# Keys and values of the recurrence turned by VectorE and device memory instead of TensorE

## What is computed

```python
def wkv_scan(r, w, k, v, kk, a, s0, reverse):       # 16 heads of 64
    def step(S, inp):
        r_t, w_t, k_t, v_t, kk_t, a_t = inp
        sa = jnp.einsum("bhvk,bhk->bhv", S, kk_t)
        S = (S * w_t[:, :, None, :]
             - sa[..., None] * (kk_t * a_t)[:, :, None, :]
             + v_t[..., None] * k_t[:, :, None, :])
        return S, jnp.einsum("bhvk,bhk->bhv", S, r_t)
oc_f, sc_f = scan_direction(con, 0, s0, False)      # context, forwards
oc_b, sc_b = scan_direction(con, 1, s0, True)       # context, backwards
ol_f, _ = scan_direction(lat, 0, sc_f, False)       # latents go on from there
ol_b, _ = scan_direction(lat, 1, sc_b, True)
```

## Time and profile before

| | us |
|---|---|
| median of three executions | 2393.3 (2391.81 to 2393.4) |
| the profiled execution | 2391.25 |
| its span, first to last instruction | 2389.2 |
| TensorE busy in the span | 2357.6 (99%) |
| VectorE / ScalarE / GpSimd busy | 1526.6 (64%) / 558.5 (23%) / 419.0 (18%) |
| from the first transpose of turn 0 to that of turn 31 | 481.56 |

### The profile page before, as it was taken

The page is one execution under the profiler, slowest core; times in us unless marked ns, Lnnn a source line. Parts: engine busy times, 40 slices in busy tenths (PEclk is TensorE's granted clock), DMA queues, the critical chain, the costliest instruction groups (busy, mean ns, idle before and its releaser), DMA issues.

```text
span 2389.2 us, 54476 instructions
## 1 busy us (share of the span) xinstructions
PE 2357.6 (99%) x24052; PEld 2057.5 (86%) x24052; DVE 1526.6 (64%) x2964; ACT 558.5 (23%) x1289; POOL 419.0 (18%) x483
## 2 busy tenths in 40 slices
PE   8999999999999999999999999999999999999999
PEld 8999888899999998889999888488888888556558
DVE  7886674488778766744987887255555554147652
ACT  2101030111011010301111111245555554132341
POOL 1111000112011100001223320234444440100000
PEclk9999999999999999999999999999999999999999
DMA  7555544445545554545454322000000001212111
GB/s 282 185 180 193 190 178 153 165 161 205 197 162 193 178 194 176 184 151 179 176 193 162 112 80 71 1 3 3 3 3 3 3 3 38 89 53 88 53 53 71
DMA packets 40427, 285.03 MB, mean 119 GB/s; under 512 B 4544, under 2 KB 5744, under 8 KB 6272
## 3 DMA queue, kind: packets, MB, share of 16 engines
q1 hardware_dynamic: 36000, 252.83, 29.6%
q0 software_dynamic: 4192, 28.72, 3.3%
HBM read 280.48 MB, written 1.05 MB: 118 GB/s over the span
## 4 chain that ended last, share of the span: by engine, by line
PE 96%; DVE 2%; ACT 2%; issue 0%; DMA 0%; POOL 0%; SPq 0%; DVEq 0%; ACTq 0%; POOLq 0%
PE psum L696 27%; PE psum L1039 21%; PE psum L1100 12%; PE psum L1208 6%; PE psum L714 5%; PE psum L1338 4%; PE psum L1327 3%; PE psum L1340 2%; PE psum L1287 1%; PE psum L1427 1%; ACT arena L1957 1%; PE psum L1010 1%; PE psum L1274 1%; PE psum L1297 1%; PE psum L1411 1%; PE psum L1355 1%
## 5 line engine op out<-in xcount | busy, mean ns | idle before, releaser
L696 PE MATMUL psum<-arena,ring 128*128 128x256 f32 (+1 forms) x2864 | 675.2, 395 | 8.3 <-ACT arena L1735 8.0
L696 PEld LDWEIGHTS psum<-arena,ring 128*128 128x128 f32 x2864 | 541.8, 190 | 129.7 <-issue 56.5
L1039 PE MATMUL psum<-arena 128*128 128x128 f32 x2560 | 325.0, 275 | 0.0
L1039 PEld LDWEIGHTS psum<-arena 128*128 128x128 f32 x2560 | 305.1, 192 | 0.0
L1039 PE MATMUL psum<-arena,ring 128*128 128x128 f32 x1920 | 253.6, 275 | 0.0
L1039 PEld LDWEIGHTS psum<-arena,ring 128*128 128x128 f32 x1920 | 233.9, 192 | 0.2
L2348 DVE TENSOR_TENSOR arena<-ring 128x1024 f32<-128x1024 f32 x136 | 171.1, 1258 | 38.6 <-PE psum L1100 34.7
L1100 PE MATMUL psum<-arena 128*128 128x128 f32 x1408 | 184.6, 275 | 0.0
L1100 PEld LDWEIGHTS psum<-arena 128*128 128x128 f32 x1408 | 170.7, 192 | 0.0
L2370 DVE SCALAR_TENSOR_TENSOR arena<-arena 128x256 f32<-128x256 f32 x336 | 164.1, 530 | 5.2
L1338 PE MATMUL psum<-arena 64*64 64x64 f32 x2560 | 158.5, 223 | 0.9 <-DVE arena L2763 0.7
(11 more groups left out here) (343 smaller groups left out, 3373.1 us busy)
## 6 DMA issues: line engine op xcount, KB each, us to landing
ring<-in_weights SPq DMA_DIRECT2D x238, 1024.0 KB, 4.8
arena<-in_ada POOLq DMA_DIRECT2D x24, 1024.0 KB, 5.4
arena<-in_const POOLq DMA_DIRECT2D x1, 1312.0 KB, 6.4
arena<-in_x SPq DMA_DIRECT2D x1, 1024.0 KB, 4.8
ring<-in_weights SPq DMA_DIRECT2D x2, 512.0 KB, 6.7
arena<-in_ctx POOLq DMA_DIRECT2D x1, 1024.0 KB, 7.5
arena<-in_lora POOLq DMA_DIRECT2D x1, 1024.0 KB, 5.2
out<-arena SPq DMA_DIRECT2D x8, 128.0 KB, 1.9
```

Source lines behind the costliest of these rows:

```text
L696: mm = self.nc.tensor.matmul(out, self.ring[:, slot % RING, i * P:(i + 1) * P], rhs, start=(kc == 0), stop=(kc == len(moving) - 1))
L1039: mm = nc.tensor.matmul(bank[:, n * P:(n + 1) * P], left[:, kind, pair, :], right[:, pair, :], start=(n == 0 and pair == 0), stop=(n == la ...
```

## The change

VectorE turns the operands in squares of 32x32, and transfers through device memory bring the squares to their partitions.

- `turn_squares(q)` on VectorE: two directions, each one transpose of the keys (128x256) and one of the values (128x128), written to `squares_turned` with a step of four elements. The backward values are read backwards from `rkv`, so `v_rev`, `reverse_values` and the memset of its head are gone.
- Where: `turn_squares(0)` stands ahead of the loop. In turns with g other than 0, `turn_squares(q+1)` stands between `take_z` and `mask_lower(q+1, 2)`; with g = 0, after `sum_decays`, `mask_lower` and `update_state`, at the end of the turn. It waits until the squares of the turn before have been spilled.
- On SP, for each turn: four transfers of 32 partitions x 6 x 128 elements (98 KB each) to `squares_0` or `squares_1` in device memory, a wait for all four, then one of 128x512 elements (262 KB) to `bk_t` and one of 64x512 (131 KB) to `uv`. From turn 2 on the latter two wait for `os_full` of the turn two before.
- TensorE loses `turned_bk` and `turned_v`; `kv` waits for the values' transfer in place of ScalarE, and the first `out_and_state` of a turn has a wait for the keys' transfer added. ScalarE loses `take_turned_bk`, `take_turned_v` and `reverse_values`.
- `bk_t` and `uv` are now `[buffer, feature, unit]`: a matrix operand reads 64 columns with a step of four elements (16 bytes), and `take_u` writes so.
- The first weight loads over `bk` are issued from between the turns' transfers and wait for `squares_turned` and `stack_full`.

```diff
-    bk_t = second.take(2, 4, P)
-    uv = second.take(2, 4, P)
+    bk_t = second.take(2, P, 4)
+    uv = second.take(2, P, 4)
     kv_buf = (second.take(4 * HEAD), second.take(4 * HEAD))
+    squares_turned = Arena(arena, second.at).take(6, SQUARE, 4)
...
+            for q in range(TURNS):
+                b, n = q % 2, q // 2 + 1
+                if q >= 2:
+                    sp.wait_ge(s.bk_landed[b], 16 * (n - 1))
+                    sp.wait_ge(s.v_landed[b], 16 * (n - 1))
+                sp.wait_ge(s.squares_turned, q + 1)
+                for f in range(P // SQUARE):
+                    rows = slice(f * SQUARE, (f + 1) * SQUARE)
+                    sp.dma_start(spilled[b][:, :, f, :].rearrange("c i t -> i c t"),
+                                 squares_turned[rows, :, :, :].rearrange("p c j u -> p c (j u)"))\
+                        .then_inc(s.squares_spilled[b], 16)
+                sp.wait_ge(s.squares_spilled[b], 4 * 16 * n)
+                if q >= 2:
+                    sp.wait_ge(s.os_full, 2 * q - 2)
+                sp.dma_start(bk_t[:, b, :, :].rearrange("p f u -> p (f u)"),
+                             spilled[b][0:4].rearrange("c i f t -> (c i) (f t)")).then_inc(s.bk_landed[b], 16)
+                sp.dma_start(uv[CHUNK:P, b, :, :].rearrange("p f u -> p (f u)"),
+                             spilled[b][4:6].rearrange("c i f t -> (c i) (f t)")).then_inc(s.v_landed[b], 16)
+                for i in range(2):
+                    if q == TURNS - GROUPS + 1 + i:
+                        load_b(i)
+            for i in range(2, SECOND_B_SLOTS):
+                load_b(i)
...
-            def turned_bk(q):
-
-                pair, g = divmod(q, GROUPS)
-                out_ = st.bank(("bk_turned", q), 512)
-                for u in range(4):
-                    jj, d = divmod(u, 2)
-                    mm = nc.tensor.transpose(out_[:, u * P:(u + 1) * P], bk[:, pair % 2, d, 2 * g + jj, :], identity)
...
-                        pe.wait_ge(s.act_taken, SCAN.taken(("v_turned", q)))
+                        pe.wait_ge(s.v_landed[q % 2], 16 * (q // 2 + 1))
                         for u in range(4):
                             jj, d = divmod(u, 2)
                             for h in range(2):
                                 mm = mm_(out_[halves[h], u * HEAD:(u + 1) * HEAD], gram_at(q % 2, jj, d, h)[HEAD:P, 0:CHUNK],
-                                         uv[HEAD:P, q % 2, u, h * HEAD:(h + 1) * HEAD], start=True, stop=True)
+                                         uv[HEAD:P, q % 2, h * HEAD:(h + 1) * HEAD, u], start=True, stop=True)
...
+                if jj == 0:
+                    pe.wait_ge(s.bk_landed[par], 16 * (q // 2 + 1))
...
-                        mm_(ps_o[halves[h], d, :], uv[:, par, 2 * jj + d, h * HEAD:(h + 1) * HEAD],
+                        mm_(ps_o[halves[h], d, :], uv[:, par, h * HEAD:(h + 1) * HEAD, 2 * jj + d],
                             gram_at(par, jj, d, h)[:, CHUNK:], start=False, stop=True)
                 for d in range(2):
                     for h in range(2):
                         cols = slice(h * HEAD, (h + 1) * HEAD)
-                        mm = mm_(ps_s[halves[h], d, :], bk_t[:, par, 2 * jj + d, cols], uv[:, par, 2 * jj + d, cols],
+                        mm = mm_(ps_s[halves[h], d, :], bk_t[:, par, cols, 2 * jj + d], uv[:, par, cols, 2 * jj + d],
...
-                turned_bk(q)
-                turned_v(q)
...
-            def reverse_values(n):
-                nc.scalar.activation(v_rev[:, n % 2, CHUNK:].rearrange("p (s t) -> p s t", s=2),
-                                     rkv[:, 2 * DC + n, :].rearrange("p (s t) -> p s t", s=2)[:, :, ::-1],
-                                     ACT.Copy).then_inc(s.reversed_ready, 1)
...
-                        uv[0:CHUNK, q % 2, 2 * jj:2 * jj + 2, h * HEAD:(h + 1) * HEAD],
+                        uv[0:CHUNK, q % 2, h * HEAD:(h + 1) * HEAD, 2 * jj:2 * jj + 2].rearrange("p f u -> p u f"),
...
-                take_turned_bk(q)
-                take_turned_v(q)
...
+            def turn_squares(q):
+                pair, g = divmod(q, GROUPS)
+                if g == 0:
+                    dve.wait_ge(s.pair_ready, pairs_ready(pair, 1))
+                if q >= 1:
+                    dve.wait_ge(s.squares_spilled[(q - 1) % 2], 4 * 16 * ((q - 1) // 2 + 1))
+                stream, at = g // 2, g % 2 * 2 * CHUNK
+                for d in range(2):
+                    nc.vector.transpose(
+                        squares_turned[:, 0:4, :, d::2].rearrange("p c j u -> p u c j"),
+                        bk[:, pair % 2, d, 2 * g:2 * g + 2, :].rearrange("p u (c j) -> p u c j", j=SQUARE))
+                    values = rkv[:, 2 * DC + pair, stream * T:(stream + 1) * T]
+                    values = (values if d == 0 else values[:, ::-1])[:, at:at + 2 * CHUNK]
+                    ins = nc.vector.transpose(
+                        squares_turned[:, 4:6, :, d::2].rearrange("p c j u -> p u c j"),
+                        values.rearrange("p (u c j) -> p u c j", u=2, c=2))
+                ins.then_inc(s.squares_turned, 1)
...
+            dve.wait_ge(s.lora_in, 4)
+            turn_squares(0)
...
+                elif ahead:
+                    turn_squares(q + 1)
                if ahead:
                    mask_lower(q + 1, 2)
                 if k >= 0:
                     update_state(k + 1)
+                if q % GROUPS == 0 and q // GROUPS + 1 < PAIRS:
+                    turn_squares(q + 1)
```

54 lines of the change are left out of this document (15 added, 39 removed).

## The result

The changed kernel takes 2435.05 us (median of four executions, 2434.45 to 2435.51) and the kernel before 2393.35 beside it. The ratio is 1.0179, with a 95% interval from 1.0167 to 1.0191. The forecast was 2388.5 in a range from 2383 to 2420; the time lies 15 us above the range. It lies nearest to rival B's figure for the case that the stationary operands are held up too, 2432. Two executions far outside all others (3432.5 us of the version with six returns, 6007.1 us of the kernel before) count in no ratio of this document.

What follows compares the result with a forecast made beforehand. TensorE's queue plus its waits for short round trips through ScalarE or VectorE bound the recurrence; -4.4 + 0.6 = -3.8 us gives 2387.4 from 2391.25 and 2389.5 from the median, middle 2388.5, range 2383 to 2420.

Steps and rivals of the forecast that it cites:

- rival B: TensorE's stepped operand reads take twice as long: 2418 us for moving operands, 2432 with stationary ones too; chance 0.26.
- the stride: TensorE operands read a float32 every 16 bytes, 48 passes a turn; ends zero and 44 us, taken as zero.
- GpSimd sets the pace: In 12 turns with g = 1 and 2, GpSimd's preparation of the next pair holds up the mask; no gain counted.
- The cover: Before lower_product(q, 4), removed transposes mostly covered ScalarE's copy; 0.23 of 1.03 us gained in 19 turns, 4.4 us.
- Turn 1: ScalarE comes late from a table load and exponentials, and lower_product follows it with or without transposes; nothing gained.
- The first turn: turn_squares(0) stands ahead of the mask, so TensorE goes on at 1556.12; 0.6 us lost, once.
- VectorE's transposes: Four a turn ahead of mask_lower(q+1, 2) take 1.4 us, ends 0.9 and 2.2, hidden in 2.3 us of room.
- rival C: VectorE's transposes don't fit and wait for GpSimd, losing 1.3 us in 14 turns: 18 us, 2407; chance 0.11.
- The transfers: Spill and return take 6.7 us, at worst 9.6, against 12.0 us from squares to kv at g = 1; zero cost.
- Rival D: Transfers land late for kv, over 12 us after turning; at 14 us seven g = 1 turns lose 2 each: 2402; chance 0.05.

Runs made afterwards that it cites:

- version with six returns: Layout by unit with each turn's two returns from device memory issued as six, one per square of tokens; 2390.4 us, ratio 0.9991 to the kernel before.
- all accesses in a row: Changed kernel with TensorE's reads of bk_t and uv and ScalarE's writes of u on neighbouring elements, values wrong; 2389.7 us, ratio 0.999 to the kernel before.
- without squares and transfers: Changed kernel with all accesses in a row, VectorE's squares and the transfers left out, values wrong; 2389.7 us, ratio 0.9989 to the kernel before.
- squares made twice: Version with six returns, with VectorE's four transposes a turn made a second time into unread memory; 2389.5 us, ratio 0.999 to the kernel before.
- layout by unit: Changed kernel with bk_t and uv kept as [buffer, unit, feature], the spill scattering 128-byte pieces; 2407.5 us, ratio 1.0064 to the kernel before.

## Why the prediction was wrong

One term of the sum was wrong, and it was as large as the whole result.

**The step that failed** is the stride: ends of zero and 44 us, zero taken. It measured 45.5 us (2435.1 against 2389.6). The reason given for zero was two rows of eight elements, a memset on VectorE, which only writes, and a small ScalarE instruction, on other engines, with a step of 256 bytes, and so short that a start-up cost of 59 or some 200 ns hides a few ns. They could not bear the choice, and the text said as much; the honest use of rows that don't reach the question is to leave both ends standing. The range did not: it cut half of rival B away to 2420, below its own figure of 2432 for the case that came. With 26% on B and a bound of 44 us, the range should have ended beyond 2432.

Rival B's price was nearly right. It took twice the time for each of 48 passes a turn, 29 ns a pass; 26 were measured for kv and for L1437. Measured from the first start of a group to whatever TensorE starts next, which takes in its last pass, kv holds the queue for 1.08 us instead of 0.59, and the two groups of `out_and_state` for 1.14 instead of 0.62 (medians): 32 x 0.49 + 64 x 0.52 = 49 us. The six turns with g = 2 in which GpSimd sets the pace gave back 0.6 us each, 3.6 in all, since TensorE's wait behind it (0.53 us in turn 14 with all accesses in a row) is gone from them in the changed kernel. That leaves 45.5 us (by unrounded medians), as much as was measured. Smaller differences (turn 2, and a stretch at half clock that the changed kernel's profile has more, told below) were not followed one by one.

**The cover** was right. TensorE waits for ScalarE's copy in place of the transposes, 0.69 us in a turn. A stretch from one `lower_product(q, 5)` to the next, in us, mean of the six turns 4 to 27 of each kind, from the starts of that line:

| | g = 0 | g = 1 | g = 2 | g = 3 |
|---|---|---|---|---|
| before | 15.90 | 16.08 | 15.12 | 15.82 |
| changed | 17.14 | 17.32 | 16.26 | 17.07 |
| changed, all accesses in a row | 15.63 | 15.81 | 15.35 | 15.55 |

With the step gone, a turn gains 0.27 us where 0.23 was forecast. That turns with g = 1 and 2 together gain nothing, since GpSimd sets the pace there, was right too: 0.27 won in the one and 0.23 lost in the other. The sum had nothing for the stride, and its 2388.5 stands against 2389.7 with all accesses in a row and 2390.4 with six returns (the kernel before had 2392.3 and 2392.0 beside them): a gain of 1.6 to 2.6 us where 3.8 were forecast.

**Turn 1 and the clock** are where the rest of the gain went. The prediction said that nothing is gained in turn 1. It loses 1.5 us: 16.47 us became 17.98 in the kernel with all accesses in a row (18.09 without squares and transfers). Up to the product that waits for ScalarE nothing has changed (12.07 us before, 12.06 then); the 1.5 us lie behind it, where TensorE's granted clock falls to 0.50 for some us. The profiled executions of all versions without a step have a second such stretch, in the first turn or at or behind the end of the recurrence, and that of the kernel before has none in the recurrence or behind it. Here is that kernel behind a wait of 3.25 us at 2121.15:

```profile
2121.30:2123.30 2.00, 2.00 (x10) 1.76 (x11) 2.00 (x6) 2.00 (x6) 0.00 (x0) 1.00 0.00 0
```

And the kernel with all accesses in a row, behind the same wait, which ends at 2116.99:

```profile
2118.00:2120.00 2.00, 2.00 (x6) 1.60 (x5) 2.00 (x4) 1.53 (x4) 0.00 (x0) 0.50 0.04 8
```

Such a stretch costs about 1.7 us: from `lower_product(30, 5)` to the end it takes 361.7 us with it and 360.0 without (the run without squares, whose second one came in its first turn). It isn't the same in each execution of a kernel. Beside the version with six returns, the kernel before took 2391.5 us in the 12 executions with a mean clock of 1.000 (median) and 2392.6 in the 17 with 0.999; the version with six returns and the one with the squares made twice had five executions with 1.000, of 2387.2 to 2388.5. At the same clock the change without a step gains 3.0 to 4.3 us, and the forecast of 3.8 lies in that. So the sum without the stride was about right, and what it lacked is the loss at half clock.

**The first turn** was right in kind. The mask now stands behind four transposes, from 1554.57 on, and starts at 1555.98; TensorE goes on at 1556.44 after 0.42 us of waiting, where 1556.12 and a loss of 0.6 were forecast. The changed kernel comes to this place 0.44 us later than the one before, for reasons ahead of the recurrence, so the loss is 0.51 us there. By `lower_product(0, 5)`, with the gain of turn 0 itself, 0.24 is left of it.

**VectorE's transposes**: 1.4 us forecast; 1.6 with stepped writes and 1.15 in a row, from the first start to the last end. Both lie inside the ends of 0.9 and 2.2, and rival C fell: no wait for the mask behind them grew.

**The transfers**: 6.7 us forecast from the squares to the landing; 6.1 to 8.0 measured in turns 0 to 29 of the changed kernel (up to 9.1 in the last two), with 12.2 us of room in the turns with g = 1 and 9.4 in turn 0, where 6.3 were needed. Rival D fell for the changed kernel and came true in the layout by unit, at 13 to 14 us.

## What to carry over

- Before a layout is turned so that one engine writes or a transfer moves it well, count for every reader how many elements of each 16 bytes it takes: on TensorE, for float32, two of four were nearly free, and one of four made the passes of 64 columns 1.7 to 1.8 times as long with one side stepped in kv and L1437, and 2.1 times with both in L1442.
- Work that stands where a queue would wait for another engine anyway is worth only what it sticks out; here 0.27 of 1.03 us a turn. The run with the work left out altogether says so in one measurement, before anything is built to replace it.
- Look at the granted clock of each execution before a difference of 2 us is explained. One stretch at half clock cost 1.7 us here, as much as the change was seen to gain.
- A price that no row of the right engine bounds belongs in the range at both ends, whatever the likeliest value is.
